# The four merge products of a hybrid attention/GLA layer, written as seven half-size block products each

## The chip, the cores and the metric

One core of a Trainium2 chip runs the whole layer as one program. Its engines work side by side, each through its own list of instructions in order: PE (TensorE: matmuls out of SBUF into PSUM banks), ACT (ScalarE), DVE (VectorE), POOL (GpSimd) and SP (SyncE, which here only issues DMAs). They wait for one another at semaphores. The metric is the device time of one execution in microseconds (us); less is better.

## The reference, cut to what matters

```python
h = rms_norm(x, g_pre_mix) * (1.0 + sc_m) + sh_m        # 1280 rows (256 context, 1024 latent) x 1024
proj = h @ w_in                                          # its last 2048 columns are `gates`
o_a = attend(q_a, k_all, v_all) @ w_pa                   # 1280x1024 @ 1024x1024
o_g = rms_norm(o_g, g_gla).reshape(B, T, GLA_V) * jax.nn.silu(r_g)
o_g = o_g @ w_pg                                         # 1280x1024 @ 1024x1024
g_a, g_b = jnp.split(jax.nn.sigmoid(gates), 2, axis=-1)  # h @ w_in[:, 4640:5664], h @ w_in[:, 5664:6688]
mix = (g_a * o_a + g_b * o_g) @ w_out
x = x + gt_m * rms_norm(mix, g_post_mix)
```

All is float32. The four merge products are the two gate products of `h` and the products with `w_pa` and `w_pg`, each 1280x1024 by 1024x1024. Attention, gated linear attention (GLA), the output projection, a router and 16 experts stand around them.

## The kernel before

The 1280 rows are ten tiles of 128 rows (t = 0 to 9). The program is a row of stages, and at most borders each engine waits until the others have finished the stage. The stages here are: attention; the first merge (`merge` with tag 0: `g_a * o_a`); GLA; the second merge (tag 1: adds `g_b * o_g`), which follows GLA on most engines without a border; the output projection; routing; experts.

A float32 product is made of three fp32r matmuls. ACT copies an operand to fp32r (the high part), DVE subtracts that copy from the original (the low part), and PE adds high·high, high·low and low·high in one PSUM bank. So each operand costs one ACT copy (`tile_high` L1126 for the rows, `W_high` L1133 for the weights) and one DVE subtraction whose two inputs both lie in SBUF (`tile_low` L1170, `W_low` L1178).

A merge has 40 steps (v, t): v = 0 and 2 are the gate products for columns 0 to 511 and 512 to 1023, v = 1 and 3 the branch products for the same columns. A step takes one row tile with all eight 128-deep chunks k of the inner dimension, so 8x3 = 24 matmuls of 128x128 by 128x512 (L1100). The row parts are double-buffered, the weight parts single: chunk k of the next v is written when the last tile of this v has used it. Four PSUM banks go round. After a gate step ACT takes the sigmoid (L1155); after a branch step DVE multiplies (L1203 or L1206), in the second merge it also adds to what the first left (L1204).

The order is written out by hand: PE, ACT and DVE each loop over the steps, one tile ahead. POOL has nothing in either merge (`pool_idle`). SP loads weights in units of 1024x512 (2 MB) into slots. The first merge's result goes to a DRAM scratch tensor, since R3 is used by GLA, and SP reads it back before the second merge (L1904). The output projection (`pe_out`) starts with a turn of tile 0, projects half of it, and turns tile 1 (L1978).

POOL does the same kind of subtraction elsewhere: in attention `stage_low` (L749) splits queries, 128x512 elements at a time, while DVE works on the softmax.

## Time and profile before

| | us |
|---|---|
| median of 3 runs (2677.54 to 2681.43) | 2680.6 |
| the profiled execution, its own time | 2678.96 |
| its span from first to last instruction | 2677.1 |
| PE busy in the span | 2538.2 |
| DVE / ACT / POOL busy | 1662.4 / 1329.9 / 285.5 |
| matmuls of the two merges (L1100) | 1920 |

### The profile page before, as it was taken

What the parts mean: (1) busy time and instruction counts of PE and PEld (TensorE: products, weight loads), DVE (VectorE), ACT (ScalarE), POOL (GpSimd) and SP (SyncE); (2) the same over time, 40 slices, a digit from 0 to 9 for tenths busy, and PEclk for the clock granted to TensorE, in tenths of its full rate; (3) what the DMA queues carried; (4) which work ended last, traced back from release to release, by engine and by line L of the source; (5) the groups of instructions that cost most, each with busy time, mean ns of one, the idle gap of its engine ahead of it and who ended that gap; (6) DMA issues with size and microseconds to landing.
All of it is one profiled execution on the core that took longest, in us unless ns stands there. A gap on an engine that the chain in (4) does not pass through costs nothing.

```text
span 2677.1 us, 37871 instructions
## 1 busy us (share of the span) xinstructions
PE 2538.2 (95%) x15199; PEld 1938.3 (72%) x15199; DVE 1662.4 (62%) x2553; ACT 1329.9 (50%) x2262; POOL 285.5 (11%) x287
## 2 busy tenths in 40 slices
PE   7999699999999999999999999996899999999994
PEld 3574499999788587676767888883677777777773
DVE  2654678886333435757576434656777767777775
ACT  3542467776423324444344332442666767666663
POOL 1441101000000001010101000000010101111012
PEclk9999899999999999999999999997899999999997
DMA  9320000000211100101012201535698888989886
GB/s 332 129 90 8 0 1 1 1 1 1 73 38 71 62 16 20 36 18 38 7 34 83 79 32 37 192 118 211 229 313 308 273 315 288 313 282 310 304 273 215
DMA packets 176608, 345.06 MB, mean 129 GB/s; under 512 B 9338, under 2 KB 37580, under 8 KB 176434
## 3 DMA queue, kind: packets, MB, share of 16 engines
q1 hardware_dynamic: 166396, 314.09, 32.9%
q0 software_dynamic: 9472, 28.32, 4.1%
q8 instruction: 121, 1.98, 0.3%
q14 instruction: 53, 0.43, 0.1%
q10 hardware_dynamic: 566, 0.24, 0.0%
HBM read 304.35 MB, written 38.27 MB: 128 GB/s over the span
## 4 chain that ended last, share of the span: by engine, by line
PE 63%; issue 22%; DMA 8%; DVE 4%; ACT 2%; POOL 1%; SPq 0%; POOLq 0%; DVEq 0%; ACTq 0%
PE ps L1100 16%; PE ps L1449 7%; PE ps L851 6%; DMA ffn_scratch<-WK 6%; PE ps L823 5%; PE ps L1409 5%; PE ps L228 4%; PE ps L1991 4%; PE ps L1512 2%; PE ps L1495 1%; PE ps L1423 1%; PE ps L2556 1%; PE ps L2017 1%; PE ps L1472 1%; PE ps L1393 1%
## 5 line engine op out<-in xcount | busy, mean ns | idle before, releaser
L2617 ACT ACTIVATE RWr<-R 128x1024 fp32r<-128x1024 f32 x384 | 377.8, 1054 | 73.6 <-PE ps L2556 69.9
L2712 DVE TENSOR_TENSOR W_low<-R,RWr 128x1024 fp32r<-128x1024 f32 x256 | 301.5, 1221 | 77.3 <-ACT RWr L2617 75.2
L2556 PE MATMUL ps<-RWr,R1r 128*128 128x512 f32 x1024 | 329.6, 396 | 6.0 <-DVE R1r L2700 4.2
L1100 PE MATMUL ps<-W_high,tile_high 128*128 128x512 f32 x640 | 250.9, 392 | 7.8 <-DVE W_low L1178 7.3
L1100 PE MATMUL ps<-W_low,tile_high 128*128 128x512 f32 x640 | 250.4, 391 | 0.0
L1100 PE MATMUL ps<-W_high,tile_low 128*128 128x512 f32 x640 | 250.4, 391 | 0.0
L2556 PEld LDWEIGHTS ps<-RWr,R1r 128*128 128x128 f32 x1024 | 193.0, 188 | 58.2 <-issue 14.2
L1170 DVE TENSOR_TENSOR tile_low<-R,tile_high 128x1024 fp32r<-128x1024 f32 x80 | 97.9, 1224 | 156.8 <-ACT tile_high L1126 156.6
L1449 PE MATMUL ps<-R3r 128*128 128x512 f32 (+1 forms) x640 | 188.5, 371 | 2.9 <-issue 2.9
L2712 DVE TENSOR_TENSOR tile_high<-R,RWr 128x1024 fp32r<-128x1024 f32 x128 | 150.9, 1220 | 29.9 <-ACT RWr L2617 29.6
L2556 PE MATMUL ps<-RWr,R3r 128*128 128x512 f32 x512 | 167.7, 399 | 0.0
L1126 ACT ACTIVATE tile_high<-R 128x1024 fp32r<-128x1024 f32 x80 | 84.5, 1056 | 143.2 <-PE ps L1100 142.8
L823 PE MATMUL ps<-W_high,R3r 128*128 128x256 f32 x768 | 152.3, 295 | 0.0
L2556 PE MATMUL ps<-W_low,R1r 128*128 128x512 f32 x384 | 150.4, 392 | 0.0
L1100 PEld LDWEIGHTS ps<-W_high,tile_high 128*128 128x128 f32 x640 | 121.1, 189 | 33.7 <-issue 7.7
L228 PE MATMUL ps<-RW,R 128*128 128x512 f32 x320 | 142.6, 599 | 0.0
L1409 PE MATMUL ps<-R,RW 128*128 128x512 f32 (+1 forms) x384 | 140.5, 521 | 0.0
L1100 PEld LDWEIGHTS ps<-W_high,tile_low 128*128 128x128 f32 x640 | 121.0, 189 | 25.4
L1100 PEld LDWEIGHTS ps<-W_low,tile_high 128*128 128x128 f32 x640 | 121.0, 189 | 25.0
L1449 PEld LDWEIGHTS ps<-R3r 128*128 128x128 f32 x640 | 116.5, 190 | 23.7 <-issue 3.7
L2507 PE MATMUL ps<-R 128*32 128x256 f32 x2048 | 122.1, 392 | 5.6 <-ACTq L2344 4.2
L1624 ACT ACTIVATE R3r<-R 128x512 fp32r<-128x512 f32 x80 | 50.0, 629 | 154.1 <-PE ps L1449 154.1
(373 smaller groups left out, 5069.8 us busy)
## 6 DMA issues: line engine op xcount, KB each, us to landing
R<-in_w_dram SPq DMA_DIRECT2D x96, 2048.0 KB, 13.3
RW<-in_w_in_dram SPq DMA_DIRECT2D x11, 1024.0 KB, 5.3
R<-in_w_mod_dram SPq DMA_DIRECT2D x5, 2048.0 KB, 14.0
RW<-in_w_in_dram SPq DMA_DIRECT2D x5, 2048.0 KB, 7.8
RW<-in_w_mod_dram SPq DMA_DIRECT2D x4, 2048.0 KB, 12.1
WK<-in_w_mod_dram SPq DMA_DIRECT2D x3, 2048.0 KB, 7.7
mix_scratch<-R SPq DMA_DIRECT2D x10, 512.0 KB, 2.6
R<-mix_scratch SPq DMA_DIRECT2D x10, 512.0 KB, 6.1
```

Source lines behind the costliest of these rows:

```text
L228: m = pe.matmul(out, lhs(k), Wslot[slot][:, k, off:off + width], start=(k == 0), stop=(k == KD - 1))
L823: m = pe.matmul(ps[:, b * 2 * P:(b + 1) * 2 * P], kT[a][:, g, b * P:(b + 1) * P], qst[g][c_][:, hp * 2 * P:(hp + 1) * 2 * P], start=(n == ...
L851: m = pe.matmul(ps[:, 7 * BANK + j * VW:7 * BANK + (j + 1) * VW], probs[u % 3][:, b, j * P:(j + 1) * P], vv[:, b, g * VW:(g + 1) * VW], st ...
L1100: i = pe.matmul(bank(m % 4), Tsplit[a][:, m % 2, k, :], Wsplit[b][:, k, :], start=(k == 0 and n == 0), stop=(k == KD - 1 and n == 2))
L1170: dve.tensor_tensor(Tsplit[1][:, m % 2, :, :], stationary(m), Tsplit[0][:, m % 2, :, :].bitcast(F32), ALU.subtract).then_inc(S("tile_split ...
L1409: m = pe.matmul(bank((2 if n == 1 else 0) + a, w), Wslot[gla_u % 2][:, k, a * DK:(a + 1) * DK], hT[:, k, c0:c0 + w], start=(k == 0), stop= ...
L1449: m = pe.matmul(bank(2 + n % 2, joint_width(h)), half[a][s][:, k % 4, :], w[b][:, k, 0:joint_width(h)], start=(k == 0 and z == 0), stop=(k ...
L1991: m = pe.matmul(bank(b), x[i][:, k, :], w[j][:, k, :], start=(k == 0 and n == 0), stop=(k == KD - 1 and n == 2))
L2507: m = pe.matmul(ps[c_ * CAP_CTX:(c_ + 1) * CAP_CTX, 4 * BANK + cols:4 * BANK + cols + CQ], x, pair_raw[i][c_ // 2][:, k, (c_ % 2) * CQ:(c_ ...
L2556: m = pe.matmul(bank(bank_of(e, i, j)), stat[a][:, k, :], w[b][:, k % 2, :], start=(k == 0 and z == 0), stop=(k == KD - 1 and z == 2))
L2617: act.activation(ring_high[n % RING], pair_raw[i][j][:, 2 * q:2 * q + 2, :], ACT.Copy).then_inc(S("weights_high"), 1)
L2712: dve.tensor_tensor(ring_low[n % RING], pair_raw[i][j][:, 2 * q:2 * q + 2, :], ring_high[n % RING].bitcast(F32), ALU.subtract).then_inc(S( ...
```

## The change

Each merge product is cut in halves: rows of a pair of tiles (2p and 2p+1; five pairs) on one side, inner dimension and columns in halves on the other. Strassen's scheme in Winograd's form then makes the four output blocks out of seven block products (combinations c = 0 to 6) in place of eight. Each product g of a merge has 35 steps (c, p) of 4x3 = 12 matmuls, so a merge has 70 steps; the first merge does the `w_pa` product and then its gate product, the second the gate product and then `w_pg`.

Four combinations need sums of row blocks (c = 2 to 5: 1, 2, 2 and 1 additions of 128x512) and four need sums of weight blocks (T1 to T4, four chunks each). POOL makes them all: 30 + 16 = 46 `tensor_tensor` of 128x512 in SBUF per product. The row sums go to four buffers. ACT and DVE split 512-wide row tiles, four buffers deep, and 28 weight chunks per product in place of 16; the weight parts of two combinations are held at a time. DVE adds the block products out of PSUM into the output blocks (L1325 to L1329), 30 per product, and multiplies by the gate in a tile buffer. In the second merge `mix` no longer comes back before the merge: POOL issues ten accumulating DMAs (L1430) that add the DRAM scratch to `mix` at the end, and the first two turns of the output projection wait for them. The weight units are loaded in another order and into both slots.

```diff
-        steps_m = [(v, t) for v in range(4) for t in range(NT)]
+        PAIRS = NT // 2
+        COMBOS, HALF_K = 7, KD // 2
+        def staggered(x, y):
+            return [(x, 0), (x, 1), (y, 0), (x, 2), (y, 1), (x, 3), (y, 2), (x, 4), (y, 3), (y, 4)]
+        ORDER = staggered(0, 1) + [(c, p) for p in range(PAIRS) for c in (2, 3)] + staggered(4, 5) + [(6, p) for p in range(PAIRS)]
+        steps_m = [(g, c, p) for g in range(2) for c, p in ORDER]
+        RAW_ROWS = {0: (0, 0), 1: (0, 1), 6: (1, 1)}
+        SUMS_AT = {2: 1, 3: 2, 4: 2, 5: 1}
+        W_SUMS = {10: [("T1", k) for k in range(HALF_K)] + [("T3", k) for k in range(HALF_K)],
+                  **{12 + k: [("T2", k)] for k in range(HALF_K)}, **{18 + 2 * k: [("T4", k)] for k in range(HALF_K)}}
+        W_SUM_OF = {2: "T1", 4: "T2", 5: "T3", 6: "T4"}
+            w_split_at[-1 if C < 1 else 0 if C < 2 else last_step[C - 2] + (3 if C == COMBOS else 0)].append(C)
...
             def pe_merge(pe, behind=()):
...
-                    for k in range(KD):
-                        if t == 0:
-                            pe.wait_ge(S("weights_split"), w0 + v * KD + k + 1)
+                    for k in range(HALF_K):
+                        if p == 0:
+                            pe.wait_ge(S("weights_split"), w0 + HALF_K * C + k + 1)
                         for n, (a, b) in enumerate(((high, high), (high, low), (low, high))):
-                            i = pe.matmul(bank(m % 4), Tsplit[a][:, m % 2, k, :], Wsplit[b][:, k, :], start=(k == 0 and n == 0), stop=(k == KD - 1 and n == 2))
+                            i = pe.matmul(bank(q % 4), row_parts[a][:, m % 4, k, :], Wsplit[b][:, HALF_K * (C % 2) + k, :],
+                                          start=(c not in (1, 5) and k == 0 and n == 0), stop=(k == HALF_K - 1 and n == 2), skip_group_check=True)
...
             def dve_merge(dve, ch, behind=()):
                 def tile_low(m):
-                    if m >= 2:
-                        dve.wait_ge(S("merge_tile_done"), m0 + m - 1)
+                    if c in RAW_ROWS:
+                        if m >= 4:
+                            dve.wait_ge(S("merge_tile_done"), m0 + m - 3)
+                        src = rows_of(g, p, *RAW_ROWS[c])
+                    else:
+                        if c == 2:
+                            dve.wait_ge(S("made_by_pool"), pooled["rows", m + 1])
+                        src = row_sums[m % 4]
                     dve.wait_ge(S("tile_high"), high0 + m + 1)
-                    dve.tensor_tensor(Tsplit[1][:, m % 2, :, :], stationary(m), Tsplit[0][:, m % 2, :, :].bitcast(F32), ALU.subtract).then_inc(S("tile_split"), 1)
+                    dve.tensor_tensor(row_parts[1][:, m % 4, :, :], src, row_parts[0][:, m % 4, :, :].bitcast(F32), ALU.subtract).then_inc(S("tile_split"), 1)
...
+                for m in range(MS + 2):
+                    if m in behind:
+                        behind[m](dve, ch)
+                    if m + 2 < MS:
+                        tile_low(m + 2)
+                    for C in w_split_at.get(m, ()):
+                        weights_low(C)
+                    if m < MS and dve_after(tag, m):
                         dve.wait_ge(S("merge_tile_done"), m0 + m + 1)
+                    for name, *at in dve_after(tag, m):
+                        (block_sum if name == "sum" else product)(*at)
...
+            def pool_merge(pool, ch):
+                def rows_sum(m):
+                    g, c, p = steps_m[m]
+                    pool.wait_ge(S("merge_tile_done"), m0 + m - 3)
+                    dst = row_sums[m % 4]
+                    if c == 2:
+                        made_here(pool.tensor_tensor(dst, a21, a22, ALU.subtract))
+                    elif c == 3:
+                        made_here(pool.tensor_tensor(dst, a12, a11, ALU.subtract))
+                        pool.wait_ge(S("made_by_pool"), n)
+                        made_here(pool.tensor_tensor(dst, dst, row_sums[(m - 1) % 4], ALU.add))
...
+                for m, (g, c, p) in enumerate(steps_m):
+                    for name, k in W_SUMS.get(m % PER, ()):
+                        weights_sum(g, name, k)
+                    if c in SUMS_AT:
+                        rows_sum(m)
...
+                    for i in range(2):
+                        for p in range(PAIRS):
+                            t = 2 * p + i
+                            pool.wait_ge(S("tiles_merged"), merged["product", 1, p, "12" if i == 0 else "21"])
+                            pool.dma_start(mix[:, t, :], mix_dram[t * P:(t + 1) * P, :], accum_op=ALU.add).then_inc(S(f"tiles_in{i}"), 16)
...
             def mix_turn(t):
+                if t < 2:
+                    pe.wait_ge(S(f"tiles_in{t}"), 16 * (len(range(t, NT, 3)) + PAIRS))
```

POOL between attention and GLA. Before, the last query split of attention is followed at once by the first instruction of GLA:

```order
85 L749 TENSOR_TENSOR W_low<-R,W_high 128x512 [waits tile_high,scores_done] x18
86 L1688 MEMSET R 1x1280 [waits stage_done_dve,stage_done_act,stage_done_pe]
87 L1689 MEMSET R 97x1024 [waits pool_chain]
88 L1690 MEMSET carry 128x512
```

Now the same place begins the first merge. RW holds the raw weights, WK the row sums; L1386 and L1390 are T2 and T4:

```order
86 L1380 TENSOR_TENSOR RW<-RW 128x512 [waits weights_landed_slot1,weights_landed_slot0,stage_done_dve,weights_split,stage_done_act,stage_done_pe]
87 L1380 TENSOR_TENSOR RW<-RW 128x512 [waits weights_split,weights_landed_slot0,weights_landed_slot1] x3
88 L1382 TENSOR_TENSOR RW<-RW 128x512 x4
89 L1404 TENSOR_TENSOR WK<-R 128x512 [waits merge_tile_done]
90 L1406 TENSOR_TENSOR WK<-R 128x512 [waits merge_tile_done]
91 L1408 TENSOR_TENSOR WK<-WK 128x512 [waits made_by_pool]
92 L1386 TENSOR_TENSOR RW<-RW 128x512 [waits made_by_pool,weights_split]
93 L1404 TENSOR_TENSOR WK<-R 128x512 [waits merge_tile_done]
94 L1386 TENSOR_TENSOR RW<-RW 128x512 [waits made_by_pool,weights_split]
95 L1406 TENSOR_TENSOR WK<-R 128x512 [waits merge_tile_done]
```

Both inputs of every one of these additions lie in SBUF, and each row sum waits until PE has finished the step four before its own.

DVE at a change of weights. Before, from v = 1 to v = 2 of the first merge:

```order
784 L1170 TENSOR_TENSOR tile_low<-R,tile_high 128x1024 [waits tile_high,merge_tile_done]
785 L1178 TENSOR_TENSOR W_low<-RW,W_high 128x512 [waits weights_high,weights_chunk_used,weights_landed_slot1]
786 L1178 TENSOR_TENSOR W_low<-RW,W_high 128x512 [waits weights_high,weights_chunk_used] x6
787 L1178 TENSOR_TENSOR W_low<-RW,W_high 128x512 [waits weights_high,merge_tile_done]
788 L1206 TENSOR_TENSOR R<-R,ps 128x512 [waits merge_tile_done,gates_made]
789 L1170 TENSOR_TENSOR tile_low<-R,tile_high 128x1024 [waits tile_high,merge_tile_done] x10
```

Now, at steps 18 to 21 of the first product, where c = 4 and c = 5 take over from 2 and 3 (L1304 is `tile_low`, L1311 `W_low`, L1325 to L1329 the block sums out of PSUM):

```order
786 L1304 TENSOR_TENSOR tile_low<-WK,tile_high 128x512 [waits tile_high]
787 L1311 TENSOR_TENSOR W_low<-RW,W_high 128x512 [waits weights_high,weights_chunk_used] x3
788 L1311 TENSOR_TENSOR W_low<-RW,W_high 128x512 [waits weights_high,merge_tile_done]
789 L1325 TENSOR_TENSOR R<-ps,R 128x512 [waits gates_made,merge_tile_done]
790 L1304 TENSOR_TENSOR tile_low<-WK,tile_high 128x512 [waits tile_high]
791 L1311 TENSOR_TENSOR W_low<-RW,W_high 128x512 [waits weights_high,weights_chunk_used] x3
792 L1311 TENSOR_TENSOR W_low<-RW,W_high 128x512 [waits weights_high,merge_tile_done]
793 L1327 TENSOR_TENSOR R<-R,ps 128x512 [waits tiles_merged,merge_tile_done]
794 L1304 TENSOR_TENSOR tile_low<-WK,tile_high 128x512 [waits tile_high]
```

In place of eight weight subtractions between two row tiles there are two groups of four, one row tile apart, and the tiles they stand between are POOL's row sums.

## Rows read from the trace of the kernel before

**Rows 1.** The page: busy time by engine, and the chain that ended last.
```profile
PE 2538.2 (95%) x15199; PEld 1938.3 (72%) x15199; DVE 1662.4 (62%) x2553; ACT 1329.9 (50%) x2262; POOL 285.5 (11%) x287
PE 63%; issue 22%; DMA 8%; DVE 4%; ACT 2%; POOL 1%; SPq 0%; POOLq 0%; DVEq 0%; ACTq 0%
```

**Rows 2.** Chain in order of time, the first merge: start us, us, what.
```profile
673.73 219.92 PE ps L1100 x960
```

**Rows 3.** Busy time in four stretches of the merges: us, engine (instructions), clock, DMA, GB/s.
```profile
674.00:784.00 110.00, 110.00 (x478) 90.85 (x478) 41.34 (x48) 36.72 (x49) 0.00 (x0) 0.98 0.14 51
784.00:894.00 110.00, 109.63 (x484) 90.49 (x482) 37.63 (x43) 30.64 (x40) 0.00 (x0) 1.00 0.20 72
...
1458.00:1560.00 102.00, 102.00 (x453) 84.44 (x452) 42.71 (x54) 32.53 (x44) 0.00 (x0) 1.00 0.15 52
1560.00:1670.00 110.00, 109.22 (x482) 90.12 (x480) 44.07 (x53) 31.26 (x41) 0.00 (x0) 1.00 0.11 39
```

**Rows 4.** Groups by line in 674:893: busy us, mean ns | idle before.
```profile
L1170 DVE TENSOR_TENSOR tile_low<-R,tile_high 128x1024 fp32r<-128x1024 f32 x39 | 47.8, 1226 | 82.2 <-ACT tile_high L1126 82.2
...
L1178 DVE TENSOR_TENSOR W_low<-RW,W_high 128x512 fp32r<-128x512 f32 x31 | 19.0, 685 | 0.0
L1133 ACT ACTIVATE W_high<-RW 128x512 fp32r<-128x512 f32 x28 | 16.1, 625 | 0.4
L1206 DVE TENSOR_TENSOR R<-R,ps 128x512 f32<-128x512 f32 x19 | 13.1, 688 | 54.1 <-PE ps L1100 54.1
```

**Rows 5.** Timeline, first merge: row copies, one per step of 24 matmuls; weight subtractions.
```profile
682.00 1.05 ACT L1126 ACTIVATE tile_high<-R 128x1024 fp32r<-128x1024 f32 x1
...
687.44 1.05 ACT L1126 ACTIVATE tile_high<-R 128x1024 fp32r<-128x1024 f32 x1
...
727.82 4.90 DVE L1178 TENSOR_TENSOR W_low<-RW,W_high 128x512 fp32r<-128x512 f32 x8
```

**Rows 6.** Timeline, POOL's 128x512 subtraction beside only small DVE instructions.
```profile
293.54 1.27 POOL L749 TENSOR_TENSOR W_low<-R,W_high 128x512 fp32r<-128x512 f32 x1 [16.25 <-ACT W_high L744]
```

**Rows 7.** Timeline, POOL and DVE in front's last tiles (L684 reads PSUM and SBUF).
```profile
238.24 2.49 POOL L749 TENSOR_TENSOR W_low<-R,W_high 128x512 fp32r<-128x512 f32 x2
238.25 1.51 DVE L684 SCALAR_TENSOR_TENSOR R<-ps,st,gqk 128x128 f32<-128x128 f32 x4 [1.12 <-POOL st L596]
239.80 1.22 DVE L697 TENSOR_TENSOR R<-R,WK 128x256 f32<-128x256 f32 x1
241.05 0.42 DVE L698 TENSOR_TENSOR R<-R,WK 128x256 f32<-128x256 f32 x1
```

**Rows 8.** Timeline, POOL's subtraction amid DVE's softmax.
```profile
359.19 2.36 DVE L939 TENSOR_TENSOR R<-R,WK 128x1024 f32<-128x1024 f32 x2 [0.68 <-ACT WK L1017]
360.48 2.22 POOL L749 TENSOR_TENSOR W_low<-R,W_high 128x512 fp32r<-128x512 f32 x1 [21.66 <-ACT W_high L744]
361.46 1.78 DVE L925 TENSOR_TENSOR WK<-RW 128x512 f32<-128x512 f32 x1
```

**Rows 9.** Timeline, the second merge's first matmuls after an idle PE.
```profile
1448.47 0.47 PE L1100 MATMUL ps<-W_high,tile_high 128*128 128x512 f32 x1 [3.54 <-DVE W_low L1178]
...
1449.90 0.63 PE L1100 MATMUL ps<-W_high,tile_low 128*128 128x512 f32 x1
1450.33 0.63 PE L1100 MATMUL ps<-W_high,tile_high 128*128 128x512 f32 x1
```

**Rows 10.** Timeline, from the second merge into the output projection.
```profile
1669.31 0.69 DVE L1203 TENSOR_TENSOR RW<-RW,ps 128x512 f32<-128x512 f32 x1 [4.03 <-PE ps L1100]
1670.03 0.69 DVE L1204 TENSOR_TENSOR R<-R,RW 128x512 f32<-128x512 f32 x1
...
1680.96 1.04 PE L1978 MATMUL ps<-ident,R 128*128 128x128 f32 x8
```

**Rows 11.** DMA issues: what, queue, count, KB each, median us to landing.
```profile
RW<-in_w_in_dram SPq DMA_DIRECT2D x5, 2048.0 KB, 7.8
...
WK<-in_x_sample_dram POOLq DMA_DIRECT2D x8, 512.0 KB, 6.7
...
out_dram<-R POOLq DMA_DIRECT2D x2, 1024.0 KB, 11.5
```

More of the change, by code:

```diff
@@ new lines, in act_after @@
+        def act_after(tag, m):
+            ops = []
+            if 0 <= m - 1 < MS and gates_role(tag, steps_m[m - 1][0]):
+                g, c, p = steps_m[m - 1]
+                ops += [("gate", g, p, b) for b in {4: ("12",), 5: ("22",), 6: ("21",)}.get(c, ())]
+            if m < MS:
+                g, c, p = steps_m[m]
+                if c == 0:
+                    ops.append(("move", g, p))
+                if c == 1 and (tag, g) != (1, 1):
+                    ops.append(("gate", g, p, "11"))
+            return ops
@@ new lines, in dve_after @@
+        def dve_after(tag, m):
+            ops = []
+            for back, when in ((2, {4: ("12",), 5: ("22",), 6: ("21",)}), (1, {1: ("11",)})):
+                if 0 <= m - back < MS and (tag, steps_m[m - back][0]) == (0, 1):
+                    g, c, p = steps_m[m - back]
+                    ops += [("product", g, p, b) for b in when.get(c, ())]
+            if m < MS:
+                g, c, p = steps_m[m]
+                for b in {2: ("22",), 3: ("12",), 4: ("12",), 5: ("22", "21"), 6: ("21",)}.get(c, ()):
+                    ops.append(("sum", g, p, b, c))
+                    if (tag, g) == (1, 1) and c >= 4 and (b, c) != ("21", 5):
+                        ops.append(("product", g, p, b))
+                if c == 1 and (tag, g) == (1, 1):
+                    ops.append(("product", g, p, "11"))
+            return ops
@@ new lines, in counted, with pool_counted @@
+        def counted(tag, after, base):
+            table = {}
+            for m in range(MS + 2):
+                for op in after(tag, m):
+                    table[op] = base + len(table) + 1
+            return table
+        def pool_counted(base):
+            table, n = {}, base
+            for m, (g, c, p) in enumerate(steps_m):
+                for name, k in W_SUMS.get(m % PER, ()):
+                    n += 1
+                    table["weights", g, name, k] = n
+                n += SUMS_AT.get(c, 0)
+                table["rows", m] = n
+            return table, n
@@ new lines, in tile_high, with weights_high @@
+                    act.activation(row_parts[0][:, m % 4, :, :], src, ACT.Copy).then_inc(S("tile_high"), 1)
+                def weights_high(C):
+                    g, c = divmod(C, COMBOS)
+                    u = u0 + 2 * g + W_BLOCK[c][1]
+                    act.wait_ge(w_full[slot[u]], w_ready[u])
+                    for k in range(HALF_K):
+                        chunk_free(act, C, k)
+                        if c in W_SUM_OF:
+                            act.wait_ge(S("made_by_pool"), pooled["weights", g, W_SUM_OF[c], k])
+                        act.activation(Wsplit[0][:, HALF_K * (C % 2) + k, :], weights_of(g, *W_BLOCK[c])[:, k, :], ACT.Copy).then_inc(S("weights_high"), 1)
@@ new lines, in act_merge @@
+                for m in range(MS + 2):
+                    if m + 2 < MS:
+                        tile_high(m + 2)
+                    for C in w_split_at.get(m, ()):
+                        weights_high(C)
+                    ops = act_after(tag, m)
+                    for name, *at in ops:
+                        if name == "gate" and at[2] != "11":
+                            gate(*at)
+                    if m < MS and steps_m[m][1] < 2:
+                        act.wait_ge(S("merge_tile_done"), m0 + m + 1)
+                    for name, *at in ops:
+                        if name == "move":
+                            move(*at)
+                        elif at[2] == "11":
+                            gate(*at)
@@ L1223, in sp_ma @@
                 load_unit(sp, u)
[L1224 to L1228 removed]
+            load_unit(sp, gla_u)
+            for i in range(2):
+                if i:
+                    load_unit(sp, gla_u + 1)
+                for p in range(PAIRS):
+                    t = 2 * p + i
+                    sp.wait_ge(S("tiles_merged"), dve_done[0]["product", 1, p, "12" if i == 0 else "21"])
+                    sp.dma_start(mix_dram[t * P:(t + 1) * P, :], mix[:, t, :]).then_inc(S("R3_moved"), 16)
         LR3 = 3 * 2 * RANK
@@ L2316, in pe_topk @@
             contexts(pe, 0, 0)
[L2317 removed]
+            pe.wait_ge(S("gates_moved"), 2)
             pe.wait_ge(S("slots_kept_act"), 1)
```

335 lines of the change are left out of this document (207 added, 128 removed).

## The prediction

> **What bounds the kernel now.** I read the page first: PE is busy 95% of the span and makes up 63% of the chain that ended last, DVE 4%, POOL 1% [rows 1]. The chain in order of time shows the first merge as one unbroken piece of 960 matmuls in 219.92 us [rows 2]; the busy time by stretch says that PE never stops in either merge (110.00 of 110.00, 109.63 of 110.00, 102.00 of 102.00), at full clock, DVE near 40% and ACT near 30% busy, POOL at nothing [rows 3]. The groups say that DVE and ACT wait for PE there and not the reverse: DVE stood 82.2 us ahead of its 39 row subtractions, by way of ACT, which itself follows PE [rows 4]. So the merges are bound by the number of matmuls, and a matmul removed is worth its pitch: two row copies one step apart start at 682.00 and 687.44, 5.44 us for 24 matmuls, 0.2267 us each [rows 5].
>
> **What goes.** 80 steps of 24 matmuls are 1920; 140 steps of 12 are 1680. 240 matmuls at 0.2267 us are 54.4 us. A new step is 2.72 us of PE, a product of 35 steps 95.2 us. If PE were fed as before, that would be the whole change.
>
> **What comes, and what it runs on.** POOL gets 46 additions of 128x512 per product. Beside small DVE instructions such an operation took 1.27 us [rows 6], two in a row 2.49 us, 1.25 each [rows 7]: 57 us of work in 95 us. DVE gets 35 row subtractions and 28 weight subtractions of 512 (0.685 us each alone, 4.90 / 8 = 0.61 in a row [rows 4, 5]), and 30 block sums out of PSUM (0.69 by L1206 [rows 4]): 38 + 21 = 59 us. Each alone fits. They don't run side by side, though. At 359.19 DVE ran two SBUF subtractions of 1.18 us; POOL's began at 360.48, just into the second, and took 2.22 us, 0.95 more than alone; DVE's next (0.69 alone) began at 361.46 and took 1.78, 1.09 more, until POOL was through [rows 8]. The same at 239.80: 1.22 us for what then took 0.42 [rows 7]. So POOL's additions and DVE's instructions with two inputs in SBUF exclude one another. Reading PSUM and SBUF, DVE is free of it: four L684 took their 1.51 us right under POOL's pair [rows 7]. Block sums are free, row and weight subtractions are not.
>
> From rows 8 a POOL operation that starts 0.95 late ends at 362.70, so it really began at 361.43, 0.12 before DVE's record ended; DVE's began at 362.55, 0.15 before POOL's ended. So one of each in turn costs 1.27 + 0.69 - 0.12 - 0.15 = 1.69 us; a further POOL operation 1.25, a further DVE one 0.61. The Trainium skill (SBUF — State Buffer, section Who interferes with whom) says that whoever issues first keeps the shared pair of ports for the whole instruction and the other fully blocks. By that rule a turn costs 1.96; the trace agrees on the blocking and shows 0.27 less. I take 1.69.
>
> **One product, step by step** (us from its step 0; unhindered, step m starts at 2.72 m). A row sum may start when the step four before has ended, so POOL's first (step 10) at 19.0, after T1 and T3.
> - Steps 10 to 13 hold 1, 2, 2 and 3 POOL operations (T2 sits in 12 to 15). The sums for 11 may start at 21.8; in the same time DVE splits the weights of c = 2 and 3, so the seven operations go in turns: 21.8 + 7 x 1.69 = 33.6. The row split of step 12 waits for the sums of 13 (the added wait for c = 2), then stands up to one POOL operation and runs 0.69: 35.0 against 32.6.
> - Steps 14 and 15 hold 5: 5 x 1.25 + 2 x 0.44 = 7.1, so 40.7; step 14 starts at 42.1 against 38.1. PE is 4 late. Steps 16 and 17 have 1 and 2 and it doesn't grow.
> - Steps 18 to 21, where c = 4 and 5 take over (the second DVE piece shown with the change). POOL's ten operations for 16 to 20 end at 40.7 + 10 x 1.25 + 5 x 0.44 = 55.4; ACT's copy and DVE's subtraction bring row tile 20 to about 57.4. Then DVE has four weight subtractions, each in turn with POOL, which may still make the sums of 21 to 23: 4 x 1.69 = 6.8, to 64.2. PE could run step 20 at 58.5, but its last three matmuls wait until 64.2: it ends at 64.9. DVE: block sum 0.69, row tile 21 (1.69) at 67; the next four weights, two in turn with the sums for 24, two free, 4.6; block sum; row tile 22 in turn: 73.6. Step 22 starts at 73.7 against 59.8.
> - Then POOL is four steps ahead, has five operations left, and PE goes at its own pace to the end. So a product ends 13.9 us late, four of them 55.6.
>
> The terms of the sum besides:
> - In the second product of each merge DVE also multiplies, ten times within c = 4 and 5, both inputs in SBUF: per step 0.61 + 1.5 x 0.65 + 0.61 = 2.2, plus two waits of about 0.6 for POOL, 3.4 against 2.72, over some five steps: +3, twice: 6. Bounds 0 and 10.
> - From one product to the next, T1 and T3 of the second collide with the split of c = 0 and 1: DVE is some 1.5 late, twice: 3. Bounds 0 and 10.
> - The end of the first merge: sum, sigmoid, product (0.69 + 0.6 + 0.69) where one multiplication of 0.69 stood: +1.4. The end of the second: sum and product for multiply and add [rows 10], equal. But turn 1 of the projection waits for the last accumulating DMA. None of this kind and size is in the trace: a plain 512 KB one from POOL's queue lands in 6.7 us, an accumulating one of 1 MB in 11.5 [rows 11]; with 1 us of issue 7.7 to 12.5 after DVE's last. DVE ended at 1670.72 and turn 1 started at 1680.96, 10.2 later [rows 10], so 0 to 2.3 of it shows. I take 1.
> - Each merge begins after the split of a half-size row tile: -0.5 each, -1. The ten reloads of `mix` by SP that go were hidden under matmuls (PE full from 1458 on [rows 3]): 0. More ACT work (35 + 28 copies of about 0.63 per product, 40 us of 95) lies beside PE: 0. Weight slots come free at about steps 24 and 28 of a product and the next split is at 32 (c = 0 of the second, whose unit takes the slot freed first), eight steps or 21.8 us later; 2 MB land in 7.8 us [rows 11]: 0.
>
> Sum: -54.4 + 55.6 + 6 + 3 + 1.4 + 1 - 1 = +11.6. Against the profiled execution's own time of 2678.96 that is 2690.6; this execution is 1.6 below the median of the runs shown, so I forecast 2692.
>
> **The rivals.**
> - *Only the sum of port work counts* (faster). If DVE's queue is never the late one, a product's end is set by POOL: 19.0 + 38 x 1.25 + 36 x 0.44 = 82.3 for its last sum, 1.9 for the split, six steps 16.3: 100.5, 5.3 late; the second product with its multiplications 8. Then -54.4 + 26.6 + 4 = -24: 2657. For it: POOL may run four steps ahead, and in rows 8 nobody starves. Against: the eight weight subtractions stand in DVE's list right ahead of the row tiles that PE needs next, and PE has a lead of two steps only.
> - *No blocking between these instructions* (faster): all is hidden, -54.4 + 4: 2630. Only rows 7 and 8 speak, and against it.
> - *The turns cost more and PE cools* (slower still). This differs from the forecast in one mechanism, what PE does while weights come in piecemeal: three matmuls (0.68 us) in every 1.7 us or more. After 3.54 us idle PE came back, and 1.4 us later its matmuls came 0.43 apart for about nine of them [rows 9], the 1.2 GHz level, 1.8 us lost. If each of eight such changes drops the clock once, +14; it decides as soon as the waits at steps 20 and 22 reach some 3.5 us. By the skill's rule of the whole instruction the 11 turns at each change would add 0.27 each, 12 us in four products, in the same direction. Either gives about 2705, both 2718.
>
> **Chances.** Forecast 0.48 (its own range 2676 to 2702), port sum 0.23, no blocking 0.06, cooling or whole-instruction turns 0.23. A measurement of this kernel can tell about 0.2%, 5.4 us, from no change. Faster by more than that takes 0.23 + 0.06 and 0.04 of the forecast's low end: 0.33. Within: 0.10 of the forecast. Slower: 0.57. The 8 in 10 range leaves out the case of no blocking and the far end of the last: 2645 to 2718.
>
> **What would show it.** Right: in each product PE stands before the first matmuls of steps 12, 20 and 22, named as waits for `W_low` or `tile_low`; 1680 matmuls at the old pitch between; POOL's additions of 1.25 us undisturbed and about 1.7 to 1.9 in the mean; DVE's subtractions of 512 well over 0.69 in the mean under POOL, the block sums at 0.69. The first merge takes some 224 us (2 x 95.2 + 2 x 13.9 + 3 + 1.5 + 1.4 - 0.5) against 220. Wrong: POOL's and DVE's durations as if alone (no blocking); PE waits of a few us in a product, all at `tile_low` (port sum); a granted clock under 0.95 in the merges (cooling); an idle PE of more than 3 us at turn 1 (the accumulating DMA).

## The result, and the profile after

The changed kernel takes 2719.9 us (2717.2 to 2722.0, median of 4 runs) beside 2680.2 us for the kernel before (4 runs on the same chip): a ratio of 1.0144, 95% interval 1.0132 to 1.0156. The forecast was 2692 us, within 2645 to 2718: the sign is right, the size is not, and the time lies 2 us above the range.

The profiled execution has a span of 2719.1 us against 2677.1. By the first matmul of each stage, the 42.0 us lie as follows: +19.7 in the first merge (674.63 to 915.21, before 673.73 to 894.58), +20.0 in the second (1471.05 to 1713.40, before 1448.47 to 1670.87), +2.0 between them, in GLA, +0.9 ahead of the first merge (the first 120 us ran at a clock of 0.91 against 0.97, and 1.0 came back later), -0.5 behind the second. With 120 matmuls fewer, each merge would be 27.2 us shorter if PE were fed as before.

The page, to be held against [rows 1]: PE is busy for less of a longer span, and in the chain that ended last DVE went from 4% to 7% and POOL from 1% to 5%.

```profile
PE 2514.6 (92%) x14959; PEld 1902.6 (70%) x14959; DVE 1855.9 (68%) x2761; ACT 1370.3 (50%) x2391; POOL 574.8 (21%) x481
...
PE 54%; issue 23%; DMA 8%; DVE 7%; POOL 5%; ACT 2%; POOLq 0%; SPq 0%; DVEq 0%; ACTq 0%
```

Busy time in stretches of the first merge (us, then PE, PEld, DVE, ACT, POOL, the granted clock, DMA), where [rows 3] had PE full throughout:

```profile
710.00:740.00 30.00, 24.78 (x99) 19.35 (x99) 20.52 (x19) 8.94 (x16) 28.89 (x21) 0.94 0.00 1
740.00:760.00 20.00, 14.25 (x51) 10.42 (x52) 17.34 (x20) 4.08 (x7) 13.38 (x9) 0.91 0.30 105
760.00:790.00 30.00, 29.93 (x133) 24.51 (x132) 24.60 (x33) 13.41 (x23) 11.36 (x9) 1.00 0.20 71
...
830.00:860.00 30.00, 25.79 (x101) 20.13 (x102) 23.24 (x21) 9.85 (x17) 28.95 (x20) 0.89 0.00 1
```

In 710 to 740 and 830 to 860 POOL is nearly full (28.9 of 30 us), in 740 to 760 DVE is (17.3 of 20). PE stands for 14 to 29% of these stretches, and the granted clock in them is 0.89 to 0.94. Where POOL has little left (760 to 790) PE is full again, at 1.00.

The groups of the first merge (busy us, mean ns | idle before and what ended it), to be held against [rows 4]:

```profile
L1208 PE MATMUL ps<-W_high,tile_high 128*128 128x512 f32 x280 | 116.3, 415 | 31.8 <-DVE tile_low L1304 20.6 <-DVE W_low L1311 8.5 <-DVE R L1329 2.4
...
L1311 DVE TENSOR_TENSOR W_low<-RW,W_high 128x512 fp32r<-128x512 f32 x56 | 61.1, 1150 | 0.0
...
L1304 DVE TENSOR_TENSOR tile_low<-WK,tile_high 128x512 fp32r<-128x512 f32 x40 | 47.1, 1182 | 19.0 <-POOL WK L1408 16.5 <-ACT tile_high L1240 2.5
L1329 DVE TENSOR_TENSOR R<-R,ps 128x512 f32<-128x512 f32 x40 | 27.4, 685 | 8.7 <-PE ps L1208 7.7 <-DVE W_low L1311 0.2
...
L1412 POOL TENSOR_TENSOR WK<-R,WK 128x512 f32<-128x512 f32 x10 | 16.2, 1618 | 0.8
```

The same subtraction that took 0.685 us takes 1.15; the block sum L1329, which reads PSUM, kept its 0.685. Steps 12 and 13, the first long wait:

```profile
709.60 0.39 PE L1208 MATMUL ps<-W_high,tile_low 128*128 128x512 f32 x1
709.87 1.26 POOL L1406 TENSOR_TENSOR WK<-R 128x512 f32<-128x512 f32 x1
711.20 1.26 POOL L1408 TENSOR_TENSOR WK<-WK 128x512 f32<-128x512 f32 x1
712.42 1.26 POOL L1386 TENSOR_TENSOR RW<-RW 128x512 f32<-128x512 f32 x1
...
712.50 1.74 DVE L1304 TENSOR_TENSOR tile_low<-WK,tile_high 128x512 fp32r<-128x512 f32 x1 [3.74 <-POOL WK L1408]
...
714.29 0.79 PE L1208 MATMUL ps<-W_high,tile_high 128*128 128x512 f32 x1 [4.30 <-DVE tile_low L1304]
...
714.88 0.63 PE L1208 MATMUL ps<-W_low,tile_high 128*128 128x512 f32 x1
715.31 0.63 PE L1208 MATMUL ps<-W_high,tile_low 128*128 128x512 f32 x1
```

DVE's row split of step 12 waits for both additions of step 13, then for POOL's next one. When PE comes back it runs at the lower of its two levels, 1.2 GHz: the granted clock of 714.29 to 717.80 is 0.56, and matmuls start 0.43 us apart instead of 0.2267, seven of them here. The change to c = 4, steps 20 and 21:

```profile
736.94 6.86 DVE L1311 TENSOR_TENSOR W_low<-RW,W_high 128x512 fp32r<-128x512 f32 x4
...
738.14 1.73 POOL L1390 TENSOR_TENSOR RW<-RW 128x512 f32<-128x512 f32 x1
...
739.83 1.73 POOL L1414 TENSOR_TENSOR WK<-R 128x512 f32<-128x512 f32 x1
740.47 0.50 PE L1208 MATMUL ps<-W_high,tile_high 128*128 128x512 f32 x1 [0.67 <-DVE W_low L1311]
...
741.52 1.73 POOL L1410 TENSOR_TENSOR WK<-R 128x512 f32<-128x512 f32 x1
```

POOL's additions start 1.69 us apart, and the four subtractions take 6.86 us, 1.715 each: one of each in turn, at the price worked out from [rows 8]. By the rule of the Trainium skill (SBUF — State Buffer, section Who interferes with whom) that a whole instruction holds the ports, it would be 1.96; the measured turns are shorter.

Between the merges the extra 2.0 us are for the most part the same thing. PE stands 2.99 us at the end of the first merge where it stood 0.94, and GLA's first matmuls then come slowly. First the changed kernel, then the one before:

```profile
915.21 8.34 PE L1602 MATMUL ps<-R,w_lr 128*32 128x512 f32 x48 [2.99 <-DVEq L223]
```

```profile
894.58 6.64 PE L1379 MATMUL ps<-R,w_lr 128*32 128x512 f32 x48 [0.94 <-DVEq L223]
```

The same 48 matmuls take 8.34 us and 6.64: 1.7 of the 2.0 us. The granted clock of 915 to 919 is 0.57 in the changed kernel.

From the starts of the matmuls of each merge come two numbers that the rest uses: *stalls*, the sum of all distances over 0.5 us less one pitch each, and *slow clock*, the excess over 0.2267 of those between 0.3 and 0.5. A *gap* at a step, below, is the distance between the step's first matmul and the one before it. Each ratio is to the kernel before as it ran beside that kernel (medians of 2678.6 to 2681.3 us).

| kernel | total, us | ratio to before (95%) | merge 1: first to last matmul, stalls, slow clock | merge 2 |
|---|---|---|---|---|
| before | 2680 | | 219.5, 0.3, 1.8 | 220.4, 0.6, 2.3 |
| changed | 2719.9 | 1.0144 (1.0132, 1.0156) | 237.2, 32.8, 13.5 | 240.4, 35.3, 14.0 |
| POOL's additions on one column | 2630.7 | 0.9820 (0.9804, 0.9836) | 194.9, 2.0, 2.6 | 193.9, 1.0, 2.5 |
| DVE's splits read PSUM | 2648.3 | 0.9883 (0.9867, 0.9900) | 203.5, 8.5, 4.6 | 200.0, 6.6, 2.8 |
| no wait for c = 2 | 2714.9 | 1.0137 (1.0120, 1.0154) | 235.4, 32.3, 12.2 | 238.6, 36.6, 11.1 |
| filler ahead of the waits | 2704.1 | 1.0097 (1.0080, 1.0114) | 230.7, 35.2, 4.6 | 231.7, 36.0, 4.5 |
| weight sums by DMA | 2676.7 | 0.9986 (0.9976, 0.9996) | 216.4, 18.5, 7.2 | 216.4, 17.5, 8.1 |
| and row sums by DVE | 2646.5 | 0.9881 (0.9865, 0.9898) | 200.6, 7.5, 2.8 | 202.6, 7.4, 4.5 |
| and two splits a step later | 2641.6 | 0.9856 (0.9841, 0.9871) | 198.0, 5.1, 2.4 | 199.2, 5.4, 2.9 |
| and behind the block sums | 2640.0 | 0.9847 (0.9834, 0.9860) | 196.6, 2.5, 3.3 | 197.6, 3.5, 3.5 |
| changed, two splits a step later | 2704.2 | 1.0089 (1.0064, 1.0114) | 227.8, 28.0, 8.7 | 234.5, 32.4, 11.1 |

840 matmuls at 0.2267 us are 190.4 us (960 are 217.6); with the stalls and the slow clock they give the first number of each cell to within 1 us. With the filler, only the distances between the useful matmuls count, so the time of the useless ones is in its stalls. The last row is the median of three executions; a fourth took 5112.9 us, for which the profiled one offers no reason, and is left out.

### The profile page after: what moved, and what is told of

The parts are those of the page before. It is cut to its first block, busy times and chain, and to the rows that moved or that the text cites. A ratio compares the mean times of both kernels' runs of the same rounds, so it can differ in the third digit from the quotient of the medians.

```text
span 2719.1 us, 38209 instructions
## 1 busy us (share of the span) xinstructions
PE 2514.6 (92%) x14959; PEld 1902.6 (70%) x14959; DVE 1855.9 (68%) x2761; ACT 1370.3 (50%) x2391; POOL 574.8 (21%) x481
## 4 chain that ended last, share of the span: by engine, by line
PE 54%; issue 23%; DMA 8%; DVE 7%; POOL 5%; ACT 2%; POOLq 0%; SPq 0%; DVEq 0%; ACTq 0%
PE ps L1208 9%; PE ps L1672 7%; DMA ffn_scratch<-WK 6%; PE ps L851 6%; PE ps L823 5%; PE ps L1632 5%; PE ps L228 4%; PE ps L2209 4%; DVE W_low L1311 2%; PE ps L1735 1%; PE ps L1718 1%; PE ps L1646 1%; PE ps L2774 1%; POOL WK L1406 1%; POOL WK L1408 1%
## 5 line engine op out<-in xcount | busy, mean ns | idle before, releaser
L1208 PE MATMUL ps<-W_high,tile_high 128*128 128x512 f32 x560 | 233.2, 416 | 66.7 <-DVE tile_low L1304 41.9
L1208 PE MATMUL ps<-W_low,tile_high 128*128 128x512 f32 x560 | 227.6, 406 | 0.0
L1208 PE MATMUL ps<-W_high,tile_low 128*128 128x512 f32 x560 | 227.2, 406 | 0.0
L1208 PEld LDWEIGHTS ps<-W_high,tile_high 128*128 128x128 f32 x560 | 111.2, 199 | 108.3 <-DVE tile_low L1304 50.0
L2679 POOL DMA_INDIRECT ffn_scratch<-WK x16 | 38.0, 2375 | 639.2 <-ACT WK L2860 639.2
L1240 ACT ACTIVATE tile_high<-WK 128x512 fp32r<-128x512 f32 x80 | 50.4, 630 | 155.4 <-POOL WK L1408 54.1
L1208 PEld LDWEIGHTS ps<-W_high,tile_low 128*128 128x128 f32 x560 | 110.8, 198 | 24.7
L1311 DVE TENSOR_TENSOR W_low<-RW,W_high 128x512 fp32r<-128x512 f32 x112 | 126.6, 1189 | 0.9 <-ACT W_high L1250 0.9
```

The costliest lines, as they stand in the source:

```text
L1208: i = pe.matmul(bank(q % 4), row_parts[a][:, m % 4, k, :], Wsplit[b][:, HALF_K * (C % 2) + k, :], start=(c not in (1, 5) and k == 0 and n ...
L1311: dve.tensor_tensor(Wsplit[1][:, HALF_K * (C % 2) + k, :], weights_of(g, *W_BLOCK[c])[:, k, :], Wsplit[0][:, HALF_K * (C % 2) + k, :].bitc ...
```

## The experiments

**POOL's time taken away.** Each addition on POOL is cut to one column:

```diff
+                def add_few(dst, a, b, op):
+                    few = (slice(None), slice(0, 1)) if len(dst.shape) == 2 else (slice(None), 0, slice(0, 1))
+                    return pool.tensor_tensor(dst[few], a[few], b[few], op)
-                        made_here(pool.tensor_tensor(r11, r11, r12, ALU.add))
+                        made_here(add_few(r11, r11, r12, ALU.add))
...
-                        src = row_sums[m % 4]
+                        src = rows_of(g, p, 0, 0)
```

> POOL's 46 additions per product are made on one column only (128x1), with every wait and signal kept, and the splits of the summed blocks read a raw row block of the same size; the sums are left out. Theory A (POOL's additions and DVE's two-input subtractions exclude one another, DVE's queue is in order, PE's clock falls after each gap): the gaps before steps 12, 20, 22, 37 and 47 go, slow matmuls fall back to some 10 per merge, L1311 and L1304 return to 0.61 to 0.69 us, about 2632 us (2680 - 54.4 + some 6). Rival B (POOL's additions are too slow by themselves, no exclusion needed): the same. Rival C (the new order is too tight for ACT and DVE alone: their 63 copies and 93 DVE operations per product, or the wait for c = 2): gaps stay at the same steps and the time stays over 2690.

Measured: 2630.7 us. The gaps at 12, 20, 22, 37, 47, 55 and 57 are gone, 14 slow matmuls are left of 77, and of the stalls only step 64 has 1.7 us. The order, the waits, the 63 copies on ACT and the 93 operations on DVE per product cost little: 48 us of the 54.4 are there against the 2678.6 us of the kernel before beside it. Rival C falls. Rival B expected the same of this run and is open until the next.

**Only the exclusion taken away.** POOL's additions are whole, DVE's subtractions of rows and weights read PSUM for the original:

```diff
-                    dve.tensor_tensor(row_parts[1][:, m % 4, :, :], src, row_parts[0]...
+                    dve.tensor_tensor(row_parts[1][:, m % 4, :, :], bank(5).rearrange("p (k n) -> p k n", k=HALF_K), row_parts[0]...
...
-                        dve.tensor_tensor(Wsplit[1]..., weights_of(g, *W_BLOCK[c])[:, k, :],
+                        dve.tensor_tensor(Wsplit[1]..., bank(5),
```

> DVE's row and weight subtractions read a PSUM bank in place of the SBUF original (the low parts are wrong), same shapes, same waits; POOL's additions are whole. Theory A: the exclusion needs two SBUF inputs on DVE, so POOL's additions fall from 1.5 to 1.7 us to 1.25, DVE's subtractions of 512 to about 0.69, and the time comes close to that of the kernel with small additions: 2632 to 2645 us. Rival B (POOL too slow by itself): the row sums alone then still end late, gaps before steps 12 and 22 stay at 2 us and more, over 2690. Rival C: as B, over 2690.

Measured: 2648.3 us, 3 us above the range given. The groups of this kernel in 674 to 870 (busy us, mean ns | idle before):

```profile
L1304 DVE TENSOR_TENSOR tile_low<-ps,tile_high 128x512 fp32r<-128x512 f32 x68 | 46.5, 686 | 54.9 <-ACT tile_high L1240 31.2 <-POOL WK L1408 23.6
L1311 DVE TENSOR_TENSOR W_low<-ps,W_high 128x512 fp32r<-128x512 f32 x56 | 34.8, 680 | 0.2 <-ACT W_high L1250 0.2
...
L1344 DVE TENSOR_TENSOR R<-R 128x512 f32<-128x512 f32 x14 | 14.2, 1017 | 3.9 <-PE ps L1208 3.7 <-DVE W_low L1311 0.2
...
L1412 POOL TENSOR_TENSOR WK<-R,WK 128x512 f32<-128x512 f32 x10 | 13.3, 1330 | 0.8
```

DVE's subtractions are back at 0.68 and POOL's additions at 1.28 to 1.35; the multiplication L1344, still with both inputs in SBUF, has 1.02 here (0.92 over all twenty, in the changed kernel 0.89; 0.69 once POOL computes nothing). So 72 us of the 89 that separate the changed kernel from the one with small additions are the exclusion, with the slow clock that follows its waits. Of the other 18 us, 15 lie in the merges: gaps of some 2 us at steps 12 and 47 and of 1.0 to 1.5 at 14 and 49, where DVE waits for POOL's sums, and a longer one at 64. Rival B (POOL too slow by itself) holds for a fifth at most, since ten multiplications of each merge still meet POOL here.

**The added wait.** The sum for c = 3 adds a raw block instead of the sum for c = 2, so that DVE's split for c = 2 needn't wait until it has been read:

```diff
-                        if c == 2:
-                            dve.wait_ge(S("made_by_pool"), pooled["rows", m + 1])
...
-                        made_here(pool.tensor_tensor(dst, dst, row_sums[(m - 1) % 4], ALU.add))
+                        made_here(pool.tensor_tensor(dst, dst, a22, ALU.add))
```

> The row sum of c = 3 adds a raw block where it added the sum of c = 2 (so it is wrong), and DVE's row split for c = 2 no longer waits for it; the number and size of all operations stay. Theory A: step 12 starts some 3 us sooner, but POOL's queue is as late as before and PE loses most of that at step 14, which needs five more additions; what is saved is mainly the slow clock after one long gap per product: 2704 to 2716 us. Rival D (the added wait is itself the cost, gap and cold restart of 6.5 us at steps 12 and 47, four times): about 2694 us and no new gap at 14.

Measured: 2714.9 us; the ratio, 1.0137, can't be told from the changed kernel's 1.0144. The gap of 4.7 us at step 12 became 0.9, 1.6 and 1.7 at 12, 13 and 15, and the gap at 20 grew from 1.1 to 3.1; stalls are 32.3 us for 32.8 in the first merge, 36.6 for 35.3 in the second. Rival D falls. The wait moved time and made none: POOL is late whether one waits for it here or two steps on.

**The slow clock by itself.** PE gets useless matmuls where it would stand:

```diff
+                fill = {12: 16, 22: 12, 37: 14, 47: 18, 57: 12, 64: 8}
                 for m, (g, c, p) in enumerate(steps_m):
+                    for _ in range(fill.get(m, 0)):
+                        W = Wsplit[0][:, HALF_K * ((COMBOS * steps_m[m - 1][0] + steps_m[m - 1][1]) % 2), :]
+                        pe.matmul(bank(7), W[:, 0:P], W, start=True, stop=True)
```

> PE gets matmuls without use ahead of its waits at steps 12, 22, 37, 47, 57 and 64 (16, 12, 14, 18, 12 and 8 of them into an unused bank, 0.2267 us each, less than the gap at each place in the first merge), so it is busy while it would stand. Theory A: the steps start when they did, since DVE and POOL set that, and the matmuls at 0.43 us after these gaps become full-speed ones: slow matmuls from some 80 to some 30 per merge, 5 to 9 us less in each, and as much as the lead of PE allows is kept: 2702 to 2712 us. Rival E (the slow matmuls don't come of PE's idleness, or PE is what the others wait for): 80 useless matmuls per merge cost up to 18 us each, 2720 to 2756 us.

Measured: 2704.1 us, with 160 matmuls more than the changed kernel. Step 12 in its timeline:

```profile
709.68 3.79 PE L1199 MATMUL ps<-W_high 128*128 128x512 f32 x16
...
714.22 0.50 PE L1212 MATMUL ps<-W_high,tile_high 128*128 128x512 f32 x1 [0.75 <-DVE tile_low L1308]
...
714.56 0.40 PE L1212 MATMUL ps<-W_low,tile_high 128*128 128x512 f32 x1
...
714.79 0.39 PE L1212 MATMUL ps<-W_high,tile_low 128*128 128x512 f32 x1
```

The step starts as late as before (39.8 us into the merge, 39.7 in the changed kernel), and at full clock. Slow matmuls fell from some 80 in each merge to some 35; 8.9 and 9.5 us of slow clock went, and the merges are 6.5 and 8.7 us shorter, since PE, now earlier, waits more at steps 14, 48 and 49 (1.7, 0.5 and 1.4 us in the first merge). The granted clock, first of the changed kernel's first merge, then of this one's, both without the start:

```profile
680.00:911.00 231.00, 202.06 (x825) 159.79 (x824) 174.87 (x191) 86.22 (x150) 140.88 (x92) 0.95 0.14 46
```

```profile
680.00:905.00 225.00, 211.23 (x907) 168.21 (x906) 173.20 (x191) 86.79 (x150) 141.88 (x92) 1.00 0.14 48
```

PE's idleness is what brought the clock down, and rival E falls.

**Sixteen of the 46 additions off POOL.** The weight sums are DMAs that accumulate inside SBUF:

```diff
-        W_SUMS = {10: [("T1", k) for k in range(HALF_K)] + [("T3", k) for k in range(HALF_K)], ...
+        W_SUMS = {10: ("T1",), 11: ("T3",), 17: ("T2",), 24: ("T4",), 28: ("free",)}
...
+                    dst, add = {"T1": (r11, r12), "T3": (r12, r22), "T2": (r22, r11), "T4": (r21, r22)}[name]
+                    pool.dma_start(dst, add, accum_op=ALU.add).then_inc(S("weights_summed"), 16)
```

> The four weight sums of a product are four accumulating DMAs inside SBUF from POOL's queue (1 MB each, one after the other), in place of 16 additions on POOL; the 30 row additions stay. Theory A: the split of c = 0 and 1 of the second product meets no POOL work, so the gap at step 37 (4.1 us and 1.8 of slow clock) goes; the gaps at 12 and 47 shrink from 4.7 and 5.3 to about 3, as T2 is out of the row sums' way; at 20 to 22 the weight splits still take turns with row sums, though POOL is four to eight additions further: some 10 us less per merge, 2695 to 2704 us. Rival F (a sum by DMA lands late, by its read and write of 1 MB over the same SBUF, 11.5 us or more each, four in a row): PE waits for W_low at steps 20 or 22 and the time doesn't fall, 2715 or more.

Measured: 2676.7 us, 18 us below the range given and within 0.3% of the kernel before. The gaps at 12 and 37 are gone, 47's has become 1.2, 0.9 and 1.1 us in steps 45 and 46, two of 0.7 and 1.1 have come inside step 11, and the ones at 20 and 22 remain (3.2 us at 22). I had credited little but the junction, the first steps of the second product. POOL's queue shows what happened at step 12, first in the changed kernel, then in this one:

```profile
704.83 1.68 POOL L1386 TENSOR_TENSOR RW<-RW 128x512 f32<-128x512 f32 x1 [2.44 <-DVE W_low L1311]
706.47 1.74 POOL L1404 TENSOR_TENSOR WK<-R 128x512 f32<-128x512 f32 x1
```

```profile
699.73 1.75 POOL L1393 TENSOR_TENSOR WK<-R 128x512 f32<-128x512 f32 x1
```

In the changed kernel the first addition of T2 (L1386) waits 2.44 us for DVE's split of the weights that it overwrites, and the row sums of steps 12 and 13 wait behind it; with T2 out of the queue the sum of step 12 starts at 699.73, not 706.47, which is 4.1 us sooner counted from the start of each merge (672.01 and 674.63). The DMA issues of 674 to 880 (KB each, us to landing) speak against rival F:

```profile
RW<-RW POOLq DMA_DIRECT2D x8, 1024.0 KB, 6.9
```

**No addition on POOL.** The row sums go to DVE as well, four steps ahead, behind its block sums:

```diff
                     for name, *at in dve_after(tag, m):
                         (block_sum if name == "sum" else product)(*at)
+                    if m + 4 < MS:
+                        rows_sum(m + 4)
```

> As the kernel with the weight sums by DMA, and the 30 row additions of a product are made by DVE itself, four steps ahead, after its block sums: POOL computes nothing in a merge. DVE has 123 operations of some 0.66 us in the first product of a merge, 81 us of 95, and 143 in the second, 94 us. Theory A (what costs is the exclusion, not the amount of work): no operation over 0.69, L1304 and L1311 at their old means, gaps only where c = 4 and 5 crowd DVE's list (4 operations a step there and 8 weight splits, 5 to 8 us late in a product at most): 2636 to 2655 us, faster than the kernel before. Rival G (the longer list of DVE is as bad as POOL's turns): PE is 10 us and more behind in each product, 2670 us or more.

Measured: 2646.5 us, 1.2% below the kernel before, and all sums are made. Rival G falls. Its groups in 674 to 880:

```profile
L1307 DVE TENSOR_TENSOR W_low<-RW,W_high 128x512 fp32r<-128x512 f32 x56 | 35.1, 685 | 0.2 <-ACT W_high L1246 0.2
...
L1300 DVE TENSOR_TENSOR tile_low<-WK,tile_high 128x512 fp32r<-128x512 f32 x40 | 27.5, 687 | 0.3
...
L1367 DVE TENSOR_TENSOR WK<-R,WK 128x512 f32<-128x512 f32 x10 | 6.9, 692 | 0.3
```

DVE has 60 operations more per merge than in the changed kernel, and is busy less (164.4 us in the first merge, in the changed kernel 180.2): an addition costs 0.69 us on it, where on POOL it cost 1.25 of POOL and held DVE up by 1.0 each time it met a subtraction (1.69 for the turn less 0.69). Gaps of 2.0 us are left at 22 and 57 and of 3.8 at 64.

**Two splits a step later.** The splits of the weights for c = 5 and 6, in this kernel and in the changed one:

```diff
-            w_split_at[-1 if C < 1 else 0 if C < 2 else last_step[C - 2] + (3 if C == COMBOS else 0)].append(C)
+            w_split_at[-1 if C < 1 else 0 if C < 2 else last_step[C - 2] + (3 if C == COMBOS else int(C % COMBOS > 4))].append(C)
```

> The kernel with row sums by DVE and weight sums by DMA, with the splits of the weights for c = 5 and c = 6 one step later in ACT's and DVE's lists, so they stand behind the row split and the block sums that PE needs first. Left in that kernel: gaps of 2.0, 2.0 and 3.8 us at steps 22, 57 and 64 of the first merge, much the same in the second. Theory A (the gaps come of four weight subtractions, 2.7 us, ahead of what PE waits for in DVE's queue): steps 22 and 57 start with their first chunk, step 64 gets its block sum 2.7 us sooner: 5 to 8 us less per merge, 2632 to 2640 us. Rival G (DVE simply has too much there, whatever the order): the gap moves to the next step and the time stays within 3 us of 2646.5.

> The same shift of one step, in the changed kernel itself, with POOL's additions as they were. Theory A: at steps 22 and 57 (gaps of 3.5) a row split in turn with POOL and four weight subtractions of 1.7 us change places, so the step starts up to 5 us sooner but waits 1.1 us before each following chunk; shorter gaps cost less slow clock: 2 to 4 us less at each of the four places, and the gap at 64 (2.8, with 1.8 of slow clock) goes: 2700 to 2710 us. Rival H (POOL's row sums are the late ones at 22, so the order of DVE's list is nothing): 2716 to 2722.

Measured: 2642.0 us (2635 to 2644), above the range of 2632 to 2640. Its ratio, 0.9858 (0.9841 to 0.9876), overlaps the 0.9881 (0.9865 to 0.9898) of the kernel without the shift; the merges of the traces are 2.6 and 3.5 us shorter, where 5 to 8 were expected. The changed kernel so altered takes 2704.2 us, by the ratios (1.0089 and 1.0144) some 15 less than the changed kernel as it is, within its range. The gap at 64 went from 3.8 to 1.1 us here and from 2.8 to 0.5 there. Step 22 kept 2.0 us: in the first merge, by its timeline, it now waited for another thing in the same queue:

```profile
733.18 2.48 DVE L1307 TENSOR_TENSOR W_low<-RW,W_high 128x512 fp32r<-128x512 f32 x4
...
735.59 0.68 DVE L1325 TENSOR_TENSOR R<-R,ps 128x512 f32<-128x512 f32 x1
...
736.37 0.47 PE L1204 MATMUL ps<-W_high,tile_high 128*128 128x512 f32 x1 [1.62 <-issue]
```

Step 22 adds into the bank of step 20, so it needs that step's block sum (L1325), and this stood behind the four weight subtractions. Rival H falls: even with POOL's additions as they are, some 15 us lay in where ACT's and DVE's lists have these splits.

**The splits behind the block sums.** In DVE's list alone:

```diff
                     for C in w_split_at.get(m, ()):
-                        weights_low(C)
+                        if C % COMBOS < 5:
+                            weights_low(C)
...
                         (block_sum if name == "sum" else product)(*at)
+                    for C in w_split_at.get(m, ()):
+                        if C % COMBOS > 4:
+                            weights_low(C)
```

> As the kernel with the two splits one step later, and in DVE's list these splits (c = 5 and 6) stand behind the block sums of their step. In the trace of that kernel step 22 stood 2.0 us: the block sum of step 20, for which it waits, ran at 735.59, behind four weight subtractions that had begun at 733.18, and the step began at 736.34. Theory A (only the order in DVE's queue): the gaps of 2.0 us at steps 22 and 57 go, in both merges, 1.5 to 2 us each: 5 to 8 us less than that kernel in the same job. Rival G (DVE has too much there): the weights are late by as much and nothing is gained, within 3 us of it.

> The kernel with row sums by DVE, weight sums by DMA and the splits for c = 5 and 6 one step later, once more, beside the one in which these splits stand behind the block sums. It should come out at 2635 to 2644 us again, as before, 36 to 44 us under the kernel before.

Measured side by side: 2640.0 (2638.4 to 2640.4) and 2641.6 us (2639.9 to 2644.4). The gap at 22 is gone in both merges, as expected, that at 57 in the first, and in the second 1.0 us of it is left; but gaps of 0.6 to 1.4 us at 59 to 65 take the place, and the merges are 1.4 and 1.6 us shorter in all, where 5 to 8 us were expected of the two. That is rival G's case: order had little left to give, and from 810 to 865 DVE is busy for 53.9 of 55 us. The ratios, 0.9847 (0.9834 to 0.9860) and 0.9856 (0.9841 to 0.9871), can't be told apart. With the lowest median this version is 41 us below the kernel before and 80 below the changed one. Of the 54.4 us of matmuls saved, 13 are still missing.

## Why the prediction was right in sign and wrong in size

- *What goes, -54.4.* Right but for some 6 us. With POOL's additions cut down the kernel takes 2630.7 us, 48 less than the kernel before beside it; the rival with no blocking had 2630.
- *A turn of POOL and DVE costs 1.69 us, PSUM readers are free.* Right: additions 1.69 apart, four subtractions in 6.86 us, block sums at 0.685; and taking SBUF from DVE's inputs took 72 us off.
- *Waits, +55.6 +6 +3.* Right as a sum, but by offsetting errors, which is luck. It is 32.3 us per merge; measured 32.8 and 35.3. Step 22 of the first merge starts 77.0 us into it; step 1 starts at 5.2 where 2.7 was the unhindered time, and less these 2.5 us step 22 is 14.7 us late, beside the 13.9 forecast. Within that, step 12 stood 4.5 us where 2.4 were forecast, since POOL stood 2.44 us for T2, a wait in no term, so that the sums of step 13 were ready 1.7 us later than worked out (712.46), and DVE's split then took a whole turn, 1.74. The junction at 37 cost 3.9 and not 1.5. Step 64's 2.6 and, in the second merge, 3.5 at steps 2 and 3 (the split of the weights for c = 1 in turn with T1) were in no term. On the other side step 14 stood not at all where 1.6 us were forecast, steps 20 to 22 cost 7.6 us where 9.9 were, and the ten multiplications added next to nothing to them (7.7 us at steps 55 to 57) where 3 were given. In the second product of the first merge the stalls add up to 19.7 us beside 18.4.
- *The clock, 0 in the sum: the step that failed.* The sum priced each wait at its own length. After each gap of 2.8 us and more in the merges PE ran at the lower level for six to eleven matmuls, as in [rows 9]; the granted clock of the first merge is 0.94, which the prediction had named as the sign of cooling (under 0.95). Slow clock rose from 1.8 and 2.3 us to 13.5 and 14.0, together +23.4 us, and GLA's slow start adds 1.7, of the 28 by which the time missed the forecast. I had this mechanism as a rival, at +14, with the condition that waits reach some 3.5 us, and my own working had step 21 end near 70 and step 22 start at 73.7: the condition was met inside the forecast, and should have been in its sum. And the changes of weights were not the only places; 12, 37, 47 and 64 had it too. The filler shows it as a cause: the granted clock back at 1.00, 18.4 us less slow clock, the two merges 15.2 us shorter. For the rest of the 28 us the slow clock is counted in the trace, not taken away by a run.
- *The small terms.* The end of the first merge: PE idle 2.99 us for 0.94, +2.0, as against +1.4. The last accumulating DMA: +1 was given; turn 1 starts at 1723.48, 10.2 us after DVE's last instruction of the merge, as before, and ahead of it PE has no wait that the trace shows, so 0. The shorter start, -1: not seen apart from the slow start. The first 120 us, +1.9 by a clock of 0.91: nothing of the change lies there, and the experiments had between 0.87 and 0.97 there.
- *Rivals.* The port sum alone (2657) assumed that DVE's queue is never the late one; step 64, step 22 and the 15 us won by reordering say that it is. The chance of 0.23 for cooling belonged on the likeliest case, and the range should have reached past 2720.

Whether the turns at steps 20 and 55 could be hidden with POOL's additions kept, by splitting the weights there earlier, wasn't tried.

## What to carry over

When work is moved to an idle engine, ask what its operands share with the busy one: POOL had 40% of the time free here, yet each addition of 1.25 us held DVE up by 1.0, more than the 0.69 that DVE takes for the whole addition. A sum of waits is not the price of the waits on TensorE: price the restart beside each of them, and if your own working has such waits, take it into the sum. In a queue in order, list what each instruction's waiter needs next; moving two weight splits of each product one step later took some 15 us off the changed kernel.
